# Seven block products for the down projection of three quarters, and two roots of a norm inside the weight splits

## The reference, cut to what matters

```
h = layer_norm(ALPHA * h + y, ln_g[i, 0], ln_b[i, 0])
u = jnp.square(jax.nn.relu(h @ w_up[i])) @ w_down[i]
h = layer_norm(ALPHA * h + u, ln_g[i, 1], ln_b[i, 1])
h = h + jax.nn.sigmoid(h @ w_ple_gate[i]) * (p[i] @ w_ple[i])
```

## Time and profile before

| what | value |
|---|---|
| median of the runs | 3860.22 us (3859.77 to 3868.22, three runs) |
| the profiled execution | 3865.52 us, its span 3863.4 us |
| TensorE busy | 3597.6 us, 93% of the span |
| GpSimd busy | 2086.0 us, 54% |
| VectorE busy | 1525.5 us, 39% |
| ScalarE busy | 909.0 us, 24% |
| weights moved | 318.31 MB on the queue of SP |

### The profile page before, as it was taken

One profiled execution on the slowest core, in us unless ns is written; L12 is line 12 of the kernel. 1 busy time (PEld: TensorE's weight loads), 2 busy tenths in 40 slices (PEclk: granted clock), 3 DMA queues, 4 the chain that ended last, 5 costly groups with the idle time before them and its releaser, 6 DMA issues. The chain is left out here.

```text
span 3863.4 us, 50909 instructions
## 1 busy us (share of the span) xinstructions
PE 3597.6 (93%) x19658; PEld 2933.2 (76%) x19658; DVE 1525.5 (39%) x2601; ACT 909.0 (24%) x2424; POOL 2086.0 (54%) x1809
## 2 busy tenths in 40 slices
PE   8999997899998999999858999988999999889999
PEld 6787883687776888878756888776888878678887
DVE  5522316887255311243374221336311334531113
ACT  2333333223135110011151111134100123511101
POOL 5555540634642566656654666642666654256665
PEclk9999995988998999999978999998999999899999
DMA  3236880243221222222202222221222222122222
GB/s 134 95 111 103 100 122 32 104 116 103 105 80 52 104 98 96 90 89 87 87 2 82 88 98 98 87 88 70 78 99 98 93 94 88 55 96 95 98 98 77
DMA packets 96733, 346.76 MB, mean 90 GB/s; under 512 B 27414, under 2 KB 46230, under 8 KB 61720
## 3 DMA queue, kind: packets, MB, share of 16 engines
q1 hardware_dynamic: 84176, 318.31, 27.5%
q10 hardware_dynamic: 12360, 25.70, 1.9%
HBM read 320.90 MB, written 18.87 MB: 88 GB/s over the span
## 5 line engine op out<-in xcount | busy, mean ns | idle before, releaser
L319 POOL TENSOR_TENSOR wl<-raw,wh 128x512 fp32r<-128x512 f32 x1076 | 1388.9, 1322 | 21.8
L315 POOL CAST wh<-raw 128x1024 fp32r<-128x1024 f32 x538 | 558.2, 1067 | 1418.1 <-PE bank L360 1106.1
L358 PE MATMUL bank<-XTh,wh 128*128 128x512 f32 (+1 forms) x2448 | 951.0, 388 | 39.7 <-DVE XTl L1207 15.1
L359 PE MATMUL bank<-XTh,wl 128*128 128x512 f32 (+1 forms) x2448 | 936.4, 383 | 0.0
L360 PE MATMUL bank<-XTl,wh 128*128 128x512 f32 (+1 forms) x2448 | 936.0, 382 | 0.0
L358 PEld LDWEIGHTS bank<-XTh,wh 128*128 128x128 f32 x2448 | 468.8, 191 | 149.1 <-issue 26.5
L360 PEld LDWEIGHTS bank<-XTl,wh 128*128 128x128 f32 x2448 | 468.0, 191 | 89.5
L359 PEld LDWEIGHTS bank<-XTh,wl 128*128 128x128 f32 x2448 | 468.6, 191 | 84.0
L359 PE MATMUL bank<-wh,HTl 128*128 128x512 f32 x1024 | 403.4, 394 | 0.0
L358 PE MATMUL bank<-wh,HTh 128*128 128x512 f32 x1024 | 401.7, 392 | 0.0
L360 PE MATMUL bank<-wl,HTh 128*128 128x512 f32 x1024 | 397.5, 388 | 0.0
(11 more groups left out here) (374 smaller groups left out, 4012.5 us busy)
## 6 DMA issues: line engine op xcount, KB each, us to landing
raw<-in_weights SPq DMA_DIRECT2D x270, 1024.0 KB, 4.8
B<-bias_d ACTq DMA_DIRECT2D x8, 1024.0 KB, 5.6
B<-bias_a ACTq DMA_DIRECT2D x8, 512.0 KB, 13.2
bias_d<-O SPq DMA_DIRECT2D x16, 256.0 KB, 21.0
MO<-HS SPq DMA_DIRECT2D x64, 64.0 KB, 2.7
bc<-in_ln_g ACTq DMA_DIRECT2D x8, 512.0 KB, 6.4
bc<-in_ln_b ACTq DMA_DIRECT2D x8, 512.0 KB, 7.6
X<-in_x SPq DMA_DIRECT2D x4, 512.0 KB, 8.1
```

What stands on the lines that cost most here:

```text
L315: x = pool.tensor_copy(wh[s][:, half], raw[r][:, half])
L319: x = pool.tensor_tensor(wl[s][:, quarter], raw[r][:, quarter], wh[s][:, quarter].bitcast(F32), ALU.subtract)
L358: nc.tensor.matmul(psum, sh, mh, start=first, stop=False)
L359: nc.tensor.matmul(psum, sl, mh, start=False, stop=False)
```

## The change

In quarters 0 to 2 of each layer the down product is computed by blocks. The hidden activations A (tokens x 1024) and the weights B (1024 x 1024) are each cut in 2 x 2 blocks, and C = A B is formed from seven products of blocks in place of eight:

A11 B11, S1 T1, S2 T2, S4 B22, S3 T3, A12 B21, A22 T4, where S1 to S4 are sums and differences of blocks of A, and T1 to T4 of blocks of B (T1 = B12 - B11, T2 = B22 - T1, T3 = B22 - B12, T4 = B21 - T2; S2, S3 and S4 are built with the matching signs).

- A product is 2 blocks of 128 tokens (j) x 4 steps x 3 matmuls = 24 matmuls. A quarter has 7 x 24 = 168 of them for the down product, where there were 192.
- The A side: for each pair of up tiles VectorE makes the sums (lines 1419 to 1423), ScalarE rounds four high parts and VectorE makes four low parts (line 1408). The first of the low parts for S1, A12 and A22 is 128 x 768 and has both inputs in SBUF.
- The B side: B11, B22 and B21 are split by GpSimd as before. T1, T2 and T3 are made by GpSimd (`w_sum`, line 1045) and T4 by VectorE (`last_w_sum`, line 1437), all in the space of `X`. ScalarE rounds their high parts (128 x 2048) and VectorE makes their low parts (line 1432, 128 x 2048, both inputs in SBUF).
- There is a third pair of `wh`/`wl`; in these quarters item i of the 11 of a quarter (4 up chunks, 7 block products) may be split once item i - 3 has been used. The two `raw` buffers stay. B11 and B12 must both be there for T1; the load of B22 follows T1, and that of B21 follows T3.
- VectorE adds each product into its blocks of C: 20 additions of 128 x 512 in a quarter (8 before), and three additions of 128 x 1024 of `U2` after quarter 2.
- ScalarE copies ALPHA * X to `Y` before quarter 0, loads the second norm's vectors later into the first one's space, and issues the load of `pT` after the up tiles of quarter 3. `R` lies in `pT`.
- The four quarters stand one after another in the program, where quarters 1 and 2 were a loop.
- In both norms the roots of blocks 1 and 3 are taken in the middle of the split of a chunk (`middle`), after two of its four subtractions.

```diff
-        def split_chunk(pool, c, r, s):
+        def split_chunk(pool, c, r, s, middle=None):
...
-            for quarter in pieces(4):
+            for n, quarter in enumerate(pieces(4)):
+                if n == 2 and middle is not None:
+                    middle()
...
+        PRODUCTS = ((A11, (4, 5)), (S1, (6, 7)), (S2, (2, 3)), (S4, (6, 7)), (S3, (0, 1)), (A12, (4, 5)), (A22, (0, 1)))
+        NEEDS = {A11: 1, S1: 2, S2: 3, S4: 3, S3: 4, A12: 2, A22: 2}
...
+                        def split_for(q, n, k):
+                            i = 11 * q + n
+                            if i > 2:
+                                pool.wait_ge(w_used.h, used0 + i - 2)
+                            landed(k)
...
+                        def seven(q):
+                            k = cu + 8 * q
+                            even, odd = raw[k % RAW], raw[1 - k % RAW]
+                            for j in (2, 3):
+                                split_for(q, j, k + j).then_inc(w_split.h, 1)
+                            x = split_for(q, 4 + B11, k + 4)
+                            landed(k + 5)
...
+                            w_sum(q, 0, odd, even)
+                            pool.sem_inc(w_split.h, 1)
+                            landed(k + 6)
+                            w_sum(q, 1, even, W_SUM[0])
+                            pool.wait_ge(*at("w_dve", 5 * q + 1))
+                            w_sum(q, 2, even, odd)
+                            pool.sem_inc(w_high.h, 1)
+                            pool.sem_inc(w_split.h, 1)
+                            split_for(q, 4 + B22, k + 6).then_inc(w_split.h, 1)
+                            split_for(q, 4 + B21, k + 7).then_inc(w_split.h, 1)
+                            for j in range(2):
+                                split_for(q + 1, j, k + 8 + j).then_inc(w_split.h, 1)
...
                         split(0, 3)
                         for norm in range(2):
                             root(norm, 0)
-                            split(32 * norm + 3, 1)
-                            root(norm, 1)
+                            split_around(32 * norm + 3, lambda: root(norm, 1))
                             root(norm, 2)
-                            split(32 * norm + 4, 1)
-                            root(norm, 3)
-                            split(32 * norm + 5, 4 if norm else 30)
+                            split_around(32 * norm + 4, lambda: root(norm, 3))
...
+                        def product(q, n):
+                            a, banks = PRODUCTS[n]
+                            (h, x) = SLOTS[(11 * q + 4 + n) % 3]
+                            if n in (B11, B22, B21):
+                                arrived(pe, 8 * q + cu + 4 + (0, 0, 0, 2, 0, 3)[n])
+                            else:
+                                pe.wait_ge(*at("w_dve", 5 * q + {T1: 1, T2: 2, T3: 3, T4: 5}[n]))
+                            for j in range(2):
...
+                                    r = three(b, ((ah, al), (h[:, c], x[:, c])), k == 0, k == 3)
+                                r.then_inc((w_used if j else tile2_done).h, 1)
...
+                        def w_high_part(q, n):
...
+                            act.wait_ge(w_used.h, used0 + i - 2)
+                            nc.scalar.activation(SLOTS[i % 3][0][:, :], W_SUM[k % 2], ACT.Copy).then_inc(rest["w_act"].h, 1)
...
+                        def w_low_part(q, n):
...
+                            v.tensor_tensor(x[:, :], W_SUM[k % 2], h[:, :].bitcast(F32), ALU.subtract).then_inc(rest["w_dve"].h, 1)
...
+                            for i in range(3):
+                                pair_first(q, i)
+                                pair_second(q, i)
+                            w_low_part(q, T1)
+                            pair_first(q, 3)
+                            pair_second(q, 3)
+                            w_low_part(q, T2)
...
+                            take(q, 0)
+                            take(q, 1)
+                            w_low_part(q, T3)
+                            last_w_sum(q)
+                            take(q, 2)
+                            take(q, 3)
+                            w_low_part(q, T4)
+                            take(q, 4)
+                            take(q, 5)
```

More of the change, by code:

```diff
@@ L39 @@
 LN_EPS = 1e-5
+SEVEN_QS = 3
 SSM_T = 8
@@ L874, in build @@
         rest = {k: signal("rest_" + k) for k in (
-            "stats", "rstd", "rows", "turned", "high", "low", "relu", "square", "up_high", "up_low",
+            "stats", "rstd", "rows", "relu", "square", "up_high", "up_low", "sums", "w_sums", "w_act", "w_dve",
             "down_taken", "gate", "ple_kept", "x_new", "x_turned", "x_high", "x_low", "p_in", "p_high", "p_low", "vectors")}
+        rest.update(turned=turned_rows, high=rows_high, low=rows_low)
         DOWN_QS = 4
+        A11, S3, S2, S4, S1, A12, A22 = range(7)
+        B11, T1, T2, B22, T3, B21, T4 = range(7)
+        PRODUCTS = ((A11, (4, 5)), (S1, (6, 7)), (S2, (2, 3)), (S4, (6, 7)), (S3, (0, 1)), (A12, (4, 5)), (A22, (0, 1)))
+        NEEDS = {A11: 1, S1: 2, S2: 3, S4: 3, S3: 4, A12: 2, A22: 2}
         def layer_rest(layer, vecs, turn):
@@ L1013, in up @@
                                 if u % 2 == 0:
-                                    arrived(pe, q * 8 + (cu + u // 2))
-                                if not isinstance(q, int) or q or u >= 4:
-                                    pe.wait_ge(rest["up_low"].h, q * 8 + (rest["up_low"].base + u - 3))
-                                up_tile(q, u)
-                        def down_tile(q, half, tt, kh, late):
-                            arrived(pe, q * 8 + (cu + 4 + 2 * half + kh))
[L1021 to L1025, removed]
+                                    arrived(pe, q * 8 + cu + u // 2)
@@ L1229, in down, with up @@
-                        def down(q, first):
-                            for half in range(2):
-                                for tt in range(TT):
-                                    wait_down(dve, q, half, tt)
-                                    y, b = Y[:, tt, cols(half)], PS[4 + tt][:, :]
-                                    if first:
-                                        r = v.scalar_tensor_tensor(y, X[:, tt, cols(half)], ALPHA, b, ALU.mult, ALU.add)
+                        def up(q, u):
+                            b = up_bank(q, u)[:, :]
+                            dve.wait_ge(*at("relu", 8 * q + u + 1))
+                            v.tensor_tensor(b, R[u % 2][:, :], b, ALU.mult).then_inc(rest["square"].h, 1)
+                            dve.wait_ge(*at("up_high", 16 * q + u + 1))
+                            v.tensor_tensor(HTl[:, u, :], b, HTh[:, u, :].bitcast(F32), ALU.subtract).then_inc(rest["up_low"].h, 1)
@@ new lines, in pair_second, with summed @@
+                        def pair_second(q, i):
+                            e, o = up_bank(q, 2 * i), up_bank(q, 2 * i + 1)
+                            first, second = slice(0, 256), slice(256, 512)
+                            s1, a12, a22 = (SA[:, n, :] for n in range(3))
+                            def summed(n, r):
+                                r.then_inc(rest["sums"].h, 1)
+                                dve.wait_ge(*at("sums", 5 * (4 * q + i) + n))
+                            dve.wait_ge(*at("relu", 8 * q + 2 * i + 2))
+                            summed(1, v.tensor_tensor(SA[:, 1:3, :], halves(R[1][:, :]), halves(o[:, :]), ALU.mult))
+                            summed(2, v.tensor_tensor(s1, a22, e[:, second], ALU.add))
+                            summed(3, v.tensor_tensor(o[:, first], s1, e[:, first], ALU.subtract))
+                            summed(4, v.tensor_tensor(o[:, second], a12, o[:, first], ALU.subtract))
+                            summed(5, v.tensor_tensor(e[:, second], a22, o[:, first], ALU.subtract))
+                            low_part(q, i, 2, operands(S1, 3, i), SA[:, :, :])
+                            low_part(q, i, 3, operands(S2, 2, i), halves(o[:, :]))
+                            low_part(q, i, 4, operands(S3, 1, i), e[:, second].unsqueeze(1))
```

300 lines of the change are left out of this document (219 added, 81 removed).

## The result

The changed kernel takes 3882.97 us, median of 7 runs (3881.75 to 3884.40); beside it the kernel before took 3860.22 (3852.15 to 3869.97). The ratio is 1.005, interval 1.0041 to 1.006: slower by 0.5%, where 3820 was forecast. This is outside the stated range of 3790 to 3868 and near the slower rival's 3888. The profiled execution has a span of 3881.1 us.

The account below looks back on a forecast made before the run. The number of TensorE matmuls was taken to bound the up and down quarters. Profiled 3865.5 - 48.4 (products less waits) - 1.5 (roots) + 10 (clock) = 3825.6, about 3820 us as a median; range 3790 to 3868.

Parts of the forecast that it names:

- the slower rival: GpSimd's sums T at 5.0 us: B22 waits of 6.0 us, 4 us saved, 33 of clock, 3888 us; chance 0.14.
- The step that failed: GpSimd's subtractions for T1 to T3, line 1045: 1.07 us each for 512 columns, a sum T 4.3 us.
- The clock: TensorE's clock after 12 waits of 2.0 to 2.3 us: 6 of 12 cost 1.7 us, 10 us, between 0 and 20.
- The ceiling: Twelve changed quarters without new waits: 81.6 us each, quarter 0 71.4; 19.9 us saved per layer, 80 over four layers.
- TensorE's only new wait is at the fourth product: TensorE's longest wait in each changed quarter, at the fourth product, released by GpSimd's low part of B22: 2.0 us in quarters 1 and 2.
- T1 to T4 are in time: Down products: T1, T2, T3 ready at 41.3, 52.7, 60.7 us for 49.0, 54.4, 67.3; no TensorE wait at T1 to T4.
- the load's 5 us of idle GpSimd: Between T1 and T2 GpSimd can't work while B22 loads: 0.2 us to the issue and 4.8 to landing.
- the port's 2.1 us for 2048 columns and 0.7 for 768: GpSimd's loss when VectorE reads two SBUF operands: 2.1 us per 2048 columns, 0.7 per 768, 13.3 per quarter.
- the chain itself: GpSimd's order from B11's split through T1 to T3 to B22, ready at 61.8 us, wanted at 59.8, in quarters 1 and 2.
- The forecast's 0.5 us of wait for B21: Each changed quarter: TensorE waits 0.5 us for B21, whose split ends at 73.2 us, wanted at 72.7 in quarters 1 and 2.
- The roots: Both norms, roots taken in the middle of a chunk's split: VectorE's rows wait less, -1.5 us over the kernel.

Follow-up runs that it names:

- Experiments 1 and 2: experiment 1, and three changed kernels whose T1 to T3 subtract the same columns, columns 1024 further, or one column back: 3799.95, 3884.44, 3797.89 us.
- experiment 1: Changed kernel with one spread-out column as second operand of the subtractions for T1 to T3 (wrong values): 3800.88 us, ratio to before 0.9839.
- experiment 3: Changed kernel with VectorE making T4's sum after the additions of products 3 and 4: 3855.76 us, ratio to before 0.998.
- first kernel of experiment 5: Changed kernel with ScalarE rounding the high parts of B22 and B21, GpSimd making only their low parts: 3822.44 us, ratio to before 0.9898.
- second kernel of experiment 5: Changed kernel with ScalarE rounding the high parts of B22 and B21, and T4's sum after the additions of products 3 and 4: 3807.97 us, ratio 0.9861.
- Experiment 7: Changed kernel with ScalarE's casts of B22 and B21, T3's low part after product 3's addition and T4's sum after the fourth: 3787.27 us, ratio 0.98.
- experiment 4: Changed kernel with T2 made from B12 instead of B22 (wrong value), so not waiting for B22's load: 3800.23 us, ratio to before 0.9837.

## Why the prediction was wrong

- **The step that failed** is the one that took the GpSimd subtraction at 1.07 us, from line 2600's 1.03, "nearer to the row with the same types". It measured 1.27 to 1.30, line 319's value. Experiments 1 and 2 show why the choice of row was wrong: the place of the operands matters. Line 2600 has one buffer with a spread-out second operand, and line 319 reads two buffers as line 1045 does; between these last two the types differ and the duration does not. A sum T takes 5.04 us, not 4.3.
- **How that grew.** I had B22 ready at 61.8 us; it came at 65.6. Three sums are 3 x 0.74 = 2.2; the later T3 pulled T2's low part onto itself, and that put T4's sum (2.1) into B22's split; 0.3 comes from B11's later start, and 0.9 went off since T2 shares less with T1's low part. That is 3.7 of 3.8. The same step in reverse is experiment 1, where these sums again lie as drawn, and B22 is ready 61.2 us after the quarter's start.
- **The clock.** I had half of the 12 waits at 1.7 us, 10 in all; it was all 12, at 1.3 to 2.9, 24 in all, since the waits were three times as long. Waits of 3.2 to 6.3 us lowered it every time (28 waits: after, experiment 3 and quarter 0 of the first kernel of experiment 5); those of 0.9 to 1.4 us did not (28 waits, experiments 1 and 5). Within the first group the loss doesn't grow with the wait. For the waits of 2.0 that I had forecast, the second kernel of experiment 5 has four cases: two lost 1.6 us each and two lost nothing. So "6 of 12 at 1.7" fits them, as far as four cases can say; the term failed because the waits were longer, not by its own reasoning.
- **The ceiling.** A product takes 5.49 us like a down tile before, not 5.44 like an up tile, and so do four of the eight up tiles, so a quarter has 82.2 us, not 81.6: 0.6 in each, 7 us in the kernel. Experiment 7 reaches it.
- **What was right:** that TensorE's only new wait is at the fourth product and for B22's low part; that T1 to T4 are in time; the load's 5 us of idle GpSimd; the port's 2.1 us for 2048 columns and 0.7 for 768; and the chain itself. It gives the slower rival's B22 at 65.8 (65.6 measured) and its wait at 6.0 (5.3: B22 is wanted 0.6 later). Its quarters without the clock, 87.6 and 78.4 for quarter 0, fit 89.63 - 1.9 = 87.7 and 80.91 - 2.7 = 78.2. Its 33 us of clock were 24, and its 4 us saved in the quarters were 2, so its total is nearer than its clock term. The forecast's 0.5 us of wait for B21 in each quarter never came, in experiment 1 either.
- **The roots** were taken as -1.5 and measured -2.7, with an interval from -6 to +1 (0.9984 to 1.0002): it cannot be told from nothing.

In sum: in layer 0, quarters 0 to 2 take 80.91 + 89.63 + 89.21 = 259.75 us against 254.5, 5.2 more. In all four layers together it is 1039.1 against 1017.1, 22 us more; the medians differ by 22.8.

The port's price is read from the rows above: 2.05 us lost by GpSimd whenever VectorE subtracts 2048 columns of SBUF with SBUF. The Trainium skill ("SBUF — State Buffer", section "Who interferes with whom") says that the only contention between engines is on the port pair which VectorE shares with GpSimd, and that it is an exclusive lock. The trace agrees: VectorE's operation grows too, from 2.29 to 3.00 and 3.36 us, by less than the one GpSimd subtraction of 1.3 us that was under way, while T3's low part, which began as such a subtraction ended, kept its 2.29 and GpSimd lost its 2.05 all the same. For the subtraction alone, the Trainium skill's "GPSIMD Engine Reference", section 3.1, gives 4497 ns for 2048 elements. The estimate of 1.12 us for 512 columns worked out from it fits neither of the two measured, 1.03 and 1.27, and here the measurement decides.

## What to carry to other kernels

Where a chain has several equal operations in a row and ends near a deadline, price the one operation by the row with the same placement of its operands, not the same types, and work the sum out at both ends of the bound: here 0.2 us per subtraction moved the end by 4 us, since work of another engine slid from one side of the critical piece to the other. When a freed engine still ends late, look first for what can be taken off its critical stretch (casts to a free engine, port-sharing work behind the deadline) rather than at the slow operation itself. A wait of several microseconds amid full matmul work cost its length and, here, some 2 us of clock on top, while one of about 1 us cost its length alone, and of four of 2 us two cost clock.

## What was not expected of the hardware

- GpSimd's subtraction of two 128x512 operands took 1.03 us when they started at the same column or one column apart, and when the second was a single column spread out, and 1.27 when they lay 1024 columns apart or in other buffers. Where between one and 1024 columns the change lies was not tried, nor what causes it.
- A shorter wait didn't cost less clock: in experiment 3, behind 3.24 us of wait in quarter 1 of layer 0, 24 matmuls took 8.36 us, where after 5.29 us they took 7.49; in sum over 12 waits it was 25 us against 24.
- GpSimd's casts lose as much to the port as its subtractions: 2.06 us (experiment 4) against 2.05.
